# Experts' outputs scattered to rows by token and choice, loaded back by plain transfers

## The chip, the cores and the metric

One core of a Trainium2 chip runs the whole program. The metric is device time in microseconds (us) of one execution; the figure given for a kernel is the median of its timed runs. The engines are PE (matmul), DVE (vector), ACT (scalar), POOL (GpSimd) and SP, which here only issues transfers. All DMA transfers, whichever engine issues them, run on the core's 16 DMA engines; in the profile queue q1 is SP's, q10 ACT's and q0 POOL's.

## What is computed

The reference is one inference step of a two-layer decoder trunk for 288 tokens of 1024 features (256 of a prompt, 8 times 4 of samples), in float32. Layer 0 mixes tokens by attention, layer 1 by a gated short convolution; each mixer is followed by a layer norm of `ALPHA*x + f(x)` and then by a mixture of experts. The change lies in the experts:

```python
g_val, g_idx = lax.top_k(p_group, 1)              # one of 4 groups
e_val, e_loc = lax.top_k(p_exp, EXPERT_TOPK)      # two of its 8 experts
gates = g_val * e_val / sum(e_val)
e_idx = g_idx * EXPERTS_PER_GROUP + e_loc
y[t] = sum over k of gates[t, k] * expert(e_idx[t, k], x[t])
expert(e, x) = (silu(x @ w_gate[e]) * (x @ w_up[e])) @ w_down[e]
```

Each token thus has two expert outputs, 576 rows of 1024 floats (4 KB) in a layer. There are 32 experts; the three matrices of one (1024x512, 1024x512, 512x1024) are 2 MB each.

## The kernel before, in words

**Slots.** Every expert has CAP = 64 slots, so a layer has 32 x 64 = 2048 slots in the first pass, of which the 576 token choices fill 18 on average for an expert. (If an expert gets more than 64 tokens, a branch under `If(full > 0)` runs further passes; it isn't taken here.) A token's slot number is `64*expert + rank`, and SLOTI holds it for six columns: three tiles of tokens (128, 128 and 32) times two choices.

**Rows in.** Two experts form a pair of 128 slots, 16 pairs in a layer. For a pair, DVE builds a 0/1 matrix of tokens by slots (`choose_rows`, L1033), PE multiplies it with the token numbers (L1498), DVE turns the result into indices (`find_rows`, L1052; an empty slot gets an index beyond the table), and POOL gathers the tokens' rows x_rows from DRAM by an indirect transfer of 128 indices (L546); indices beyond the bound are skipped. PE transposes them, ACT evacuates.

**An expert.** PE does gate and up together (L1475, L1478), ACT the silu (L612), DVE the product (L1111), PE a transpose (L1186), DVE its copy (L1116, `ht`), PE the down product (L1490) into one bank: 64 slots by the first 512 outputs in partitions 0 to 63, the other 512 in partitions 64 to 127. PE interleaves: gate and up of expert e, then the down product of e-1, then the transpose of e. ACT's order in a step is silu of e, evacuation of a gathered pair, output of e-1.

**Weights.** SP loads them in program order into three buffers; each load waits until the expert three before has used its buffer (`load_gate_up` L382, its gate load L387, its up load L388; `load_down` L390, load L395).

**Rows out.** ACT copies an expert's bank once, 128x512 (L762; the trace shows the helper's line L609), into one of NYO = 4 buffers YO, and issues two stores of 64x512 floats (128 KB each, L745) to the table slot_out in DRAM, which has a row for each slot, filled or empty. After all stores POOL gathers back, by SLOTI, one row for each token and choice: six indirect transfers (L593) into four buffers YG, the last two after DVE has used the first (`y_used`). Each is preceded by an `If` for the overflow table. DVE accumulates `x += gate * y` twice a tile (L1144), and norms the rows (`norm_rows`); POOL computes the power for it (L532).

**Around it.** In layer 0 SP loads two of six blocks of the convolution's weights when the down product of expert 29 is done (L445), then waits for all six gathers (L447) before it loads the other four.

Of the kernel before, what the change touches and what calls it, by code (L numbers as in the profile page):

```python
# [20 lines left out]
F32 = mybir.dt.float32  # L21
I32 = mybir.dt.int32
# [92 lines left out]
def build_in(nc, t, ctx):  # L115
# [25 lines left out]
    WORK = 9396  # L141
# [7 lines left out]
    SLOTI, SLOTM, SLOTQ, TOKI, IDXC, FLAG = common(6), common(6), common(6), common(3), common(1), common(2)  # L149
    TOKF, IDXG = common(3), common(2)  # L150
    ZERO = common(SLOTS // 128)
# [44 lines left out]
    NYO = 4  # L196
    moe = region(WORK, S0)
    HID, HT, YO, OHP = moe(2, FE), moe(2, FC, CAP), moe(NYO, D // 2), moe(2, 3, 2 * CAP)
# [5 lines left out]
    YG = region(WORK, S0)(4, D)  # L204
# [6 lines left out]
    behind_yg = region(WORK + 4 * D, S0)  # L211
    SCW, SCT, UL = behind_yg(D), behind_yg(DC, 19), behind_yg(DC, 18)
# [6 lines left out]
    table_d = nc.dram_tensor("bias_table", [SHIFTS, 17, TABLE_W], F32).ap()  # L219
    xrows_d = [nc.dram_tensor(f"x_rows{i}", [NTOK, D], F32).ap() for i in range(DEPTH)]  # L220
    slot_tok_d = [nc.dram_tensor(f"slot_token{i}", [SLOTS, 1], I32).ap() for i in range(DEPTH)]
    yslot_d = [nc.dram_tensor(f"slot_out{i}", [NE * CAP, D], F32).ap() for i in range(DEPTH)]
    ymore_d = [nc.dram_tensor(f"slot_more{i}", [SLOTS - NE * CAP, D], F32).ap() for i in range(DEPTH)]
# [28 lines left out]
    st_y = [sem(f"st_y{k}") for k in range(NYO)]  # L252
    ygath = [sem(f"ygath{k}") for k in range(4)]
# [4 lines left out]
    more = [{n: sem(f"more{i}_{n}") for n in ("scat", "w", "tok", "gath", "T", "Tevac", "gu", "silu", "h", "hT", "hTe", "dn", "y", "st", "more")} for i in range(DEPTH)]  # L258
# [34 lines left out]
    def store_count(layer, e):  # L293

        return 32 * (layer * (NE // NYO) + e // NYO + 1)

    NOWHERE = 4096
# [5 lines left out]

    def ygath_count(layer, j):

        return 16 * (layer * (2 if j % 4 < 2 else 1) + j // 4 + 1)


# [28 lines left out]
    def _(sp):  # L337
# [63 lines left out]
        def experts(layer):  # L401
# [12 lines left out]
            with sp.If(full > 0):  # L414
# [8 lines left out]
                sp.wait_ge(s["st"], 32 * n_more)  # L423
            with sp.Else():
                sp.nop()

# [19 lines left out]
        for k in range(4):  # L446
            sp.wait_ge(ygath[k], ygath_count(0, k + 4 if k < 2 else k))  # L447
# [24 lines left out]
    def _(pool):  # L472
        nc.gpsimd.memset(ZERO.bitcast(I32), NTOK).then_inc(zero_set, 1)
        nc.gpsimd.memset(NEGH, -0.5).then_inc(zero_set, 1)
        pool.wait_ge(zero_set, 2)
        nc.gpsimd.iota(TOKI.bitcast(I32), pattern=[[128, 3]], base=0, channel_multiplier=1).then_inc(zero_set, 1)
        pool.wait_ge(zero_set, 3)
        nc.gpsimd.tensor_scalar(TOKF, TOKI.bitcast(I32), float(-NOWHERE), None, ALU.add).then_inc(zero_set, 1)
# [55 lines left out]
        def experts(layer):  # L534
# [7 lines left out]
            for q in range(NPAIR):  # L542
# [5 lines left out]
                    in_offset=bass.IndirectOffsetOnAxis(ap=IDXG[:, q % 2:q % 2 + 1].bitcast(I32), axis=0),  # L548
                    bounds_check=NTOK - 1, oob_is_err=False).then_inc(xr_ld[q % 2], 16)
            pool.wait_ge(xg_T, NPAIR * (layer + 1))  # L550
# [3 lines left out]
            with pool.If(full > 0):  # L554
                for i, (_, n) in enumerate(TILES):
                    for k in range(2):
                        pool.indirect_dma_start(
                            out=slot_tok_d[layer], out_offset=bass.IndirectOffsetOnAxis(ap=SLOTI[0:n, 2 * i + k:2 * i + k + 1].bitcast(I32), axis=0),
                            in_=TOKI[0:n, i:i + 1].bitcast(I32), in_offset=None).then_inc(s["scat"], 16)
                pool.wait_ge(s["scat"], 96)  # L560
                with pool.Fori(1, PASSES) as r:
                    with pool.Fori(0, NE) as e:
                        n = (r - 1) * NE + e
                        pool.wait_ge(s["T"], n)
                        pool.dma_start(IDXC[0:CAP, 0:1].bitcast(I32), slot_tok_d[layer][bass.ds((r * NE + e) * CAP, CAP)]).then_inc(s["tok"], 16)
# [6 lines left out]
                pool.wait_ge(s["st"], 32 * n_more)  # L572
            with pool.Else():
                pool.nop()

            for k in range(NYO):
                pool.wait_ge(st_y[k], 32 * (NE // NYO) * (layer + 1))
            for j in range(6):
                i = STEPS[j // 2]
                n, col = TILES[i][1], 2 * i + j % 2  # L580
                if j >= 4:
                    pool.wait_ge(y_used, 6 * layer + j - 3)
                with pool.If(full > 0):

                    pool.indirect_dma_start(
                        out=YG[0:n, j % 4, :], out_offset=None, in_=ymore_d[layer],
                        in_offset=bass.IndirectOffsetOnAxis(ap=SLOTM[0:n, col:col + 1].bitcast(I32), axis=0),
                        bounds_check=SLOTS - NE * CAP - 1, oob_is_err=False).then_inc(s["more"], 16)
                    pool.wait_ge(s["more"], 16 * (j + 1))
                with pool.Else():  # L590
                    pool.nop()

                pool.indirect_dma_start(  # L593
                    out=YG[0:n, j % 4, :], out_offset=None, in_=yslot_d[layer],
                    in_offset=bass.IndirectOffsetOnAxis(ap=SLOTI[0:n, col:col + 1].bitcast(I32), axis=0),
                    bounds_check=NE * CAP - 1, oob_is_err=False).then_inc(ygath[j % 4], 16)
# [9 lines left out]
    def _(act):  # L606
# [133 lines left out]
        def experts(layer):  # L740
# [46 lines left out]
            for k in range(NYO):  # L787
                act.wait_ge(st_y[k], 32 * (NE // NYO) * (layer + 1))
# [844 lines left out]
```

## Time and profile before

| | us |
|---|---|
| median of 3 timed runs (1528.38 to 1538.88) | 1536.95 |
| the profiled execution | 1526.45 |
| its span, first to last instruction | 1524.8 |

The profile is of one execution. The expert stage of layer 0 runs from about 309 to 788 us of the span, that of layer 1 from about 1001 to 1486 us. Between them lies the convolution. "Idle" in a row is what the engine waited before these instructions, and what ended it. A matmul row's line is that of the kernel; ACT's copies all carry the helper's line L609.

### The profile page before, as it was taken

Reading aid. Unit: us, or ns where it says so; the run is one execution under the profiler, and the core shown is the slowest. Engines: PE = TensorE matmul, PEld = TensorE weight load, DVE = VectorE, ACT = ScalarE, POOL = GpSimd, SP = SyncE. Lnnn points to the kernel's source line nnn. Section 1 sums busy time; section 2 is a strip of 40 time slices with the busy share of each in tenths; the row PEclk is TensorE's granted clock in tenths of the full one; section 3 lists DMA queues with packets and bytes.
Section 4 is the critical chain, followed back from the end, with each engine's and each line's share of the span. In section 5 each row is a group of like instructions: output and inputs, shape, how many; then the busy total and the mean of one; then the engine's idle time right before and its main releaser. Section 6 shows DMA issues by size and latency. Waiting matters only on the chain.

```text
span 1524.8 us, 14763 instructions
## 1 busy us (share of the span) xinstructions
PE 1280.9 (84%) x5744; PEld 588.1 (39%) x5744; DVE 329.7 (22%) x1056; ACT 201.1 (13%) x457; POOL 103.9 (7%) x149
## 2 busy tenths in 40 slices
PE   6999899599988888889864998689989898898880
PEld 4766445333333233233223774333333233333320
DVE  0053525521111111111004323421111111111005
ACT  1123431021111101101000000021101011011100
POOL 4001310100000000000001000000000000000002
PEclk9999999699999999999986999779989999999995
DMA  8740544969999999999989234549999999999973
GB/s 224 197 166 21 166 146 187 374 249 424 420 419 424 420 422 423 420 423 419 425 320 325 79 158 182 207 145 423 419 423 421 419 423 419 424 419 422 421 293 100
DMA packets 100403, 488.33 MB, mean 320 GB/s; under 512 B 14799, under 2 KB 19935, under 8 KB 83948
## 3 DMA queue, kind: packets, MB, share of 16 engines
q1 hardware_dynamic: 80772, 452.70, 73.2%
q0 software_dynamic: 8256, 15.02, 4.1%
q10 hardware_dynamic: 11304, 19.65, 3.5%
q8 instruction: 47, 0.77, 0.2%
q14 instruction: 24, 0.20, 0.0%
HBM read 476.93 MB, written 22.44 MB: 328 GB/s over the span
## 4 chain that ended last, share of the span: by engine, by line
PE 46%; DMA 37%; SPq 7%; DVE 4%; issue 2%; POOL 1%; ACT 1%; POOLq 0%; ACTq 0%; DVEq 0%
DMA mem<-w_exp_up 34%; PE bank L1478 9%; PE bank L1475 7%; SPq L387 7%; PE bank L1591 6%; PE bank L1225 5%; PE bank L1326 4%; PE bank L1490 4%; PE bank L1186 3%; PE bank L1223 1%; DMA mem<-w_attn_in 1%; PE bank L1363 1%; PE bank L1429 1%; ACT mem L609 1%; DMA mem<-slot_out,mem 1%
## 5 line engine op out<-in xcount | busy, mean ns | idle before, releaser
L1478 PE MATMUL bank<-mem 128*64 128x512 f32 x1024 | 500.9, 646 | 97.7 <-DMA mem<-w_exp_up 97.7
L1475 PE MATMUL bank<-mem 128*64 128x512 f32 x1024 | 510.2, 648 | 3.7 <-ACT mem L609 3.0
L1478 PEld LDWEIGHTS bank<-mem 128*64 128x64 f32 x1024 | 146.4, 148 | 362.2 <-issue 220.0
L1490 PE MATMUL bank<-mem 128*64 128x512 f32 x1024 | 240.3, 601 | 2.1 <-DVE mem L1116 2.1
L609 ACT COPY mem<-bank 128x512 f32<-128x512 f32 (+8 forms) x275 | 127.3, 491 | 587.3 <-PE bank L1490 195.6
L1186 PE MATMUL bank<-mem 128*128 128x128 f32 (+4 forms) x798 | 120.4, 285 | 73.3 <-DVE mem L980 37.7
L1111 DVE TENSOR_TENSOR mem<-mem,bank 64x512 f32<-64x512 f32 x64 | 44.3, 692 | 623.6 <-ACT mem L612 623.6
L1475 PEld LDWEIGHTS bank<-mem 128*64 128x64 f32 x1024 | 142.7, 148 | 73.2 <-issue 64.3
L1186 PEld LDWEIGHTS bank<-mem 128*128 128x128 f32 (+4 forms) x798 | 89.6, 165 | 168.5 <-issue 89.1
L612 ACT ACTIVATE mem<-bank 64x512 f32<-64x512 f32 x64 | 37.7, 589 | 638.2 <-PE bank L1478 638.2
L1490 PEld LDWEIGHTS bank<-mem 128*64 128x64 f32 x1024 | 70.3, 137 | 120.8 <-issue 114.4
L1591 PE MATMUL bank<-mem 128*128 128x288 f32 x384 | 95.3, 412 | 0.7 <-ACT mem L609 0.7
L546 POOL DMA_INDIRECT mem<-x_rows,mem x32 | 31.9, 995 | 808.7 <-DVE mem L1057 779.9
L1591 PEld LDWEIGHTS bank<-mem 128*128 128x128 f32 x384 | 74.1, 193 | 21.8 <-ACT mem L609 1.1
L1225 PE MATMUL bank<-mem 128*128 128x288 f32 (+1 forms) x288 | 78.3, 430 | 2.3 <-DMA mem<-w_attn_in 2.3
L1116 DVE COPY mem<-bank 128x256 f32<-128x256 f32 x64 | 27.2, 425 | 208.4 <-PE bank L1186 208.4
L1225 PEld LDWEIGHTS bank<-mem 128*128 128x128 f32 (+1 forms) x288 | 55.6, 197 | 21.5 <-issue 4.1
L1326 PE MATMUL bank<-mem 128*128 128x512 f32 x128 | 61.5, 636 | 0.0
L1498 PEld LDWEIGHTS bank<-mem 128*128 128x128 f32 (+1 forms) x192 | 28.4, 203 | 30.0 <-issue 28.9
L1326 PEld LDWEIGHTS bank<-mem 128*128 128x128 f32 x128 | 25.7, 207 | 30.7 <-issue 30.6
L1498 PE MATMUL bank<-mem 128*128 128x1 f32 (+1 forms) x192 | 31.6, 268 | 6.3 <-DVE mem L1048 6.3
L532 POOL TENSOR_TENSOR mem<-mem 128x1 f32<-128x1 f32 (+1 forms) x12 | 18.1, 1506 | 236.1 <-DVE mem L976 236.0
(172 smaller groups left out, 589.9 us busy)
## 6 DMA issues: line engine op xcount, KB each, us to landing
mem<-w_exp_gate SPq DMA_DIRECT2D x64, 2048.0 KB, 33.6
mem<-w_exp_up SPq DMA_DIRECT2D x64, 2048.0 KB, 31.7
mem<-w_exp_down SPq DMA_DIRECT2D x64, 2048.0 KB, 35.8
slot_out<-mem ACTq DMA_DIRECT2D x128, 128.0 KB, 7.6
mem<-w_conv_in SPq DMA_DIRECT2D x6, 2048.0 KB, 17.8
mem<-w_attn_in SPq DMA_DIRECT2D x5, 2048.0 KB, 16.6
mem<-w_attn_out SPq DMA_DIRECT2D x1, 4096.0 KB, 16.5
mem<-cache_k_a SPq DMA_DIRECT2D x16, 256.0 KB, 2.7
```

Source lines behind the costliest of these rows:

```text
L387: sp.dma_start(WG[k], t["w_exp_gate"][layer, e].rearrange("(p c) f -> p c f", c=DC)).then_inc(ld_wg[k], 16)
L609: return nc.scalar.copy(out, in_)
L612: return nc.scalar.activation(out, in_, ACT.Silu)
L1111: V_.tensor_tensor(h, h, bank[2 + k][CAP:2 * CAP, :], ALU.mult).then_inc(h_done, 1)
L1186: return nc.tensor.transpose(out, in_, ID[0:n, 0:n] if n is not None else ID[CAP:2 * CAP, CAP:2 * CAP])
L1225: last = mm(out[0:n, 0:NTOK], w[:, c, :], XT[:, c, :], start=c == 0, stop=c == DC - 1)
L1326: last = mm(bank[2 * i + half][0:n, :], rows, w[:, c, 512 * half:512 * half + 512], start=c == 0, stop=c == DC - 1)
L1475: mm(out[0:CAP, :], x[:, c, :], wg[:, c, :], start=c == 0, stop=c == DC - 1)
L1478: last = mm(out[CAP:2 * CAP, :], x[:, c, :], wu[:, c, :], start=c == 0, stop=c == DC - 1)
L1490: last = mm(out[CAP * half:CAP * half + CAP, :], h[:, f, :], wd[:, f, 512 * half:512 * half + 512], start=f == 0, stop=f == FC - 1)
L1498: last = mm(bank[q % 2][:, 0:1], OHP[0:n, q % 2, j, :], TOKF[0:n, j:j + 1], start=j == 0, stop=j == 2)
L1591: last = mm(bank[3 * (j % 2) + part][:, 0:NTOK], w[:, c, 128 * (j % 4):128 * (j % 4) + 128], XT[:, c, :], start=c == 0, stop=c == DC - 1)
```

## The change

Instead of storing every slot, the kernel writes only the filled slots' rows, to a table y_rows with a row for each token and choice, by an indirect transfer from POOL with 128 indices for each pair; empty slots get an index beyond the bound and are left out. For this the one-hot matrix holds 1 for a first choice and 2 for a second, and PE multiplies it with two columns (token number less an offset, and 1), so that DVE can tell the choice (HITS) and derive both the index to gather and the row to write (IDXY). ACT copies an expert's bank in two halves so that a pair's 128 slots lie in 128 partitions with 4 KB each, in two buffers YP. POOL's scatters follow its gathers with a lag of three pairs. Back come six plain loads from SP into six buffers YG, with no branch; the table is in token order. SLOTM, the overflow table and its gathers go; the overflow branch scatters too. The convolution's small inputs SCW move into free partitions of X, as YG takes their place.

The core of the diff:

```diff
-    YG = region(WORK, S0)(4, D)
+    YG = region(WORK, S0)(6, D)
...
+    ROW0, ROW1, NROWS, NOWHERE = 2 * NTOK + 1, 1, 3 * NTOK + 1, 4 * NTOK + 1
...
+    def token_rows(table, k, lo, n):
+        if k == 0:
+            return table[ROW0 + lo:ROW0 + lo + n]
+        return table[ROW1:ROW1 + 2 * NTOK].rearrange("(t two) d -> t two d", two=2)[lo:lo + n, 0, :]
...
+        def load_outputs(layer):
+            for k in range(NYP):
+                sp.wait_ge(st_y[k], store_count(layer, NPAIR - NYP + k))
+            for j in range(6):
+                i = STEPS[j // 2]
+                lo, n = TILES[i]
+                sp.dma_start(YG[0:n, j, :], token_rows(yrows_d[layer], j % 2, lo, n)).then_inc(ld_y[j], 16)
...
         load_conv(0, (0, 1))
-        for k in range(4):
-            sp.wait_ge(ygath[k], ygath_count(0, k + 4 if k < 2 else k))
+        load_outputs(0)
         load_conv(0, (2,))
         load_conv(1)
...
         experts(1)
+        load_outputs(1)
...
-            for q in range(NPAIR):
+            def gather(q):
                 Q = NPAIR * layer + q
                 pool.wait_ge(ix_ready, Q + 1)
                 wait(pool, xg_T, Q - 1)
                 pool.indirect_dma_start(
...
+            def scatter(q):
+                pool.wait_ge(y_evac, base + 2 * q + 2)
+                pool.indirect_dma_start(
+                    out=yrows_d[layer], out_offset=bass.IndirectOffsetOnAxis(ap=IDXY[:, q:q + 1].bitcast(I32), axis=0),
+                    in_=YP[:, q % NYP, :], in_offset=None,
+                    bounds_check=NROWS - 1, oob_is_err=False).then_inc(st_y[q % NYP], 16)
+            LAG = 3
+            for q in range(NPAIR):
+                gather(q)
+                if q >= LAG:
+                    scatter(q - LAG)
+            for q in range(NPAIR - LAG, NPAIR):
+                scatter(q)
...
-            for k in range(NYO):
-                pool.wait_ge(st_y[k], 32 * (NE // NYO) * (layer + 1))
-            for j in range(6):
...
-                pool.indirect_dma_start(
-                    out=YG[0:n, j % 4, :], out_offset=None, in_=yslot_d[layer],
-                    in_offset=bass.IndirectOffsetOnAxis(ap=SLOTI[0:n, col:col + 1].bitcast(I32), axis=0),
-                    bounds_check=NE * CAP - 1, oob_is_err=False).then_inc(ygath[j % 4], 16)
...
                 act.wait_ge(dn_psum, E + 1)
-                wait(act, st_y[b], store_count(layer, e) - 32)
-                copy(YO[0:2 * CAP, b, :], bank[6 + k][0:2 * CAP, :]).then_inc(y_evac, 1)
-                act.wait_ge(y_evac, E + 1)
-                store(e * CAP, yslot_d[layer], YO[0:2 * CAP, b, :], st_y[b])
+                wait(act, st_y[q % NYP], store_count(layer, q) - 16)
+                for half in range(2):
+                    last = copy(YP[CAP * k:CAP * k + CAP, q % NYP, 512 * half:512 * half + 512],
+                                bank[6 + k][CAP * half:CAP * half + CAP, :])
+                last.then_inc(y_evac, 1)
...
-            wait(dve, xr_ld[q % 2], row_loads(layer, q) - 16)
-            V_.tensor_scalar(IDXG[:, q % 2:q % 2 + 1].bitcast(I32), bank[q % 2][:, 0:1], float(NOWHERE), None,
-                             ALU.add).then_inc(ix_ready, 1)
+            found = bank[q % 2]
+            link(V_.tensor_scalar(HITS[:, q:q + 1], found[:, 1:2], -0.5, 1.5, ALU.mult, ALU.add))
+            V_.tensor_scalar(IDXG[:, q:q + 1].bitcast(I32), found[:, 0:1], HITS[:, q:q + 1], float(2 * NTOK), ALU.mult, ALU.add)
+            V_.tensor_scalar(IDXY[:, q:q + 1].bitcast(I32), found[:, 0:1], float(NOWHERE), None, ALU.add).then_inc(ix_ready, 1)
...
-                    last = mm(bank[q % 2][:, 0:1], OHP[0:n, q % 2, j, :], TOKF[0:n, j:j + 1], start=j == 0, stop=j == 2)
+                    last = mm(bank[q % 2][:, 0:2], OHP[0:n, q % 2, j, :], TOKF[0:n, j, :], start=j == 0, stop=j == 2)
```

`store_count(layer, q)` is 16 for each scatter of a pair's buffer so far; DVE's accumulates wait for `ld_y[j]` of their own load.

## Rows read from the trace of the kernel before

**Rows 1.** The page: the chain's shares by line, and the convolution's matmul group.

```profile
DMA mem<-w_exp_up 34%; PE bank L1478 9%; PE bank L1475 7%; SPq L387 7%; PE bank L1591 6%; PE bank L1225 5%; PE bank L1326 4%; PE bank L1490 4%; PE bank L1186 3%; PE bank L1223 1%; DMA mem<-w_attn_in 1%; PE bank L1363 1%; PE bank L1429 1%; ACT mem L609 1%; DMA mem<-slot_out,mem 1%
...
L1591 PE MATMUL bank<-mem 128*128 128x288 f32 x384 | 95.3, 412 | 0.7 <-ACT mem L609 0.7
```

**Rows 2.** The chain in order of time: start us, us, what.

```profile
351.65 3.58 PE bank L1490 x16
...
363.49 3.58 PE bank L1490 x16
...
1128.48 8.55 SPq L387
...
1176.28 8.34 SPq L387
```

**Rows 3.** DMA, 333 to 772 us; the last row is of 1027 to 1468 us.

```profile
DMA  9999999999999999999999999999999999999999
...
q1 hardware_dynamic: 22759, 175.22, 95.5%
q10 hardware_dynamic: 4640, 7.61, 4.6%
q0 software_dynamic: 1872, 1.77, 1.2%
...
slot_out<-mem ACTq DMA_DIRECT2D x59, 128.0 KB, 7.6
...
mem<-x_rows,mem POOLq DMA_INDIRECT x13, 9.8
...
q10 hardware_dynamic: 4660, 7.65, 4.6%
```

**Rows 4.** Windows after a gather, between gathers: busy, PE clock, DMA, GB/s.

```profile
451.00:461.00 10.00, 8.57 (x42) 2.76 (x40) 0.42 (x1) 0.58 (x1) 0.82 (x1) 1.00 1.02 415
...
461.00:482.00 21.00, 18.14 (x80) 6.71 (x78) 3.67 (x11) 2.84 (x5) 0.00 (x0) 0.92 1.02 425
```

**Rows 5.** DMA, 1000 to 1085 us: GB/s in 40 slices of 2.1 us.

```profile
GB/s 0 8 0 0 0 77 254 424 422 428 430 46 116 247 432 426 412 411 396 420 436 436 424 465 409 380 413 414 465 418 434 409 421 387 420 439 438 431 434 431
```

**Rows 6.** The chain in order of time: both tails, a first gather.

```profile
301.29 3.48 DMA mem<-x_rows,mem
...
787.61 0.59 ACT mem L609
...
802.47 1.30 DVE mem L1144
...
1484.92 0.59 ACT mem L609
...
1498.24 1.30 DVE mem L1144
```

**Rows 7.** The timeline at the first index of layer 0: start, us.

```profile
300.20 0.14 DVE L1057 TENSOR_SCALAR mem<-bank 128x1 int32<-128x1 f32 x1
```

**Rows 8.** DMA issues of the whole run: KB each, us to landing.

```profile
mem<-x_prompt SPq DMA_DIRECT2D x1, 1024.0 KB, 6.9
...
new_v_a_prompt<-mem SPq DMA_DIRECT2D x1, 512.0 KB, 2.8
...
mem<-slot_out,mem POOLq DMA_INDIRECT x12, 4.5
```

**Rows 9.** The timeline of one step of layer 1: start, us, idle before.

```profile
1117.01 0.99 POOL L546 DMA_INDIRECT mem<-x_rows,mem  x1 [30.48 <-DVE mem L1057]
...
1119.18 0.59 ACT L609 COPY mem<-bank 128x512 f32<-128x512 f32 x1 [3.85 <-PE bank L1490]
...
1119.56 0.42 DVE L1116 COPY mem<-bank 128x256 f32<-128x256 f32 x1 [3.32 <-PE bank L1186]
```

**Rows 10.** Waits, 450 to 740 us: total us, times, longest.

```profile
POOL mem L546 <- DVE mem L1057: 273.5, 9, 30.7
ACT mem L612 <- PE bank L1478: 193.6, 18, 13.7
```

More of the change, by code:

```diff
@@ L140, in build_in @@
     S0 = TOTAL - 3 * SLOT
-    WORK = 9396
+    WORK = 9536
     common = region(0, WORK)
@@ L251, in build_in @@
     xr_ld = [sem(f"xr_ld{k}") for k in range(2)]
-    st_y = [sem(f"st_y{k}") for k in range(NYO)]
-    ygath = [sem(f"ygath{k}") for k in range(4)]
+    st_y = [sem(f"st_y{k}") for k in range(NYP)]
+    ld_y = [sem(f"ld_y{j}") for j in range(6)]
     x_alpha, y_used, pe_passed, pool_passed = sem("x_alpha"), sem("y_used"), sem("pe_passed"), sem("pool_passed")
@@ L257, in build_in @@
         sem("cv_" + n) for n in ("in_T", "in", "psum", "h", "u", "z", "lT", "lsb"))
-    more = [{n: sem(f"more{i}_{n}") for n in ("scat", "w", "tok", "gath", "T", "Tevac", "gu", "silu", "h", "hT", "hTe", "dn", "y", "st", "more")} for i in range(DEPTH)]
+    more = [{n: sem(f"more{i}_{n}") for n in ("scat", "w", "tok", "gath", "T", "Tevac", "gu", "silu", "h", "hT", "hTe", "dn", "y", "st")} for i in range(DEPTH)]
     def linker(eng, own):
@@ L472, in _ @@
     def _(pool):
-        nc.gpsimd.memset(ZERO.bitcast(I32), NTOK).then_inc(zero_set, 1)
+        nc.gpsimd.memset(ZERO.bitcast(I32), NOWHERE).then_inc(zero_set, 1)
         nc.gpsimd.memset(NEGH, -0.5).then_inc(zero_set, 1)
         pool.wait_ge(zero_set, 2)
-        nc.gpsimd.iota(TOKI.bitcast(I32), pattern=[[128, 3]], base=0, channel_multiplier=1).then_inc(zero_set, 1)
+        nc.gpsimd.memset(TOKF, 1.0)
+        for k, (row, step) in enumerate(((ROW0, 1), (ROW1, 2))):
+            nc.gpsimd.iota(TOKI[:, k, :, 0].bitcast(I32), pattern=[[128, 3]], base=0, channel_multiplier=1)
+            last = nc.gpsimd.iota(TOKI[:, k, :, 1].bitcast(I32), pattern=[[128 * step, 3]], base=row, channel_multiplier=step)
+        last.then_inc(zero_set, 1)
         pool.wait_ge(zero_set, 3)
-        nc.gpsimd.tensor_scalar(TOKF, TOKI.bitcast(I32), float(-NOWHERE), None, ALU.add).then_inc(zero_set, 1)
+        nc.gpsimd.tensor_scalar(TOKF[:, :, 0], TOKI[:, 0, :, 0].bitcast(I32), float(-2 * NTOK), None, ALU.add).then_inc(zero_set, 1)
         for layer in range(DEPTH):
@@ L571, in experts @@
                             bounds_check=NTOK - 1, oob_is_err=False).then_inc(s["gath"], 16)
[L572 removed]
+                        pool.wait_ge(s["y"], n + 1)
+                        pool.sem_inc(pool_passed, 1)
+                        pool.indirect_dma_start(
+                            out=yrows_d[layer], out_offset=bass.IndirectOffsetOnAxis(ap=IDXC[0:CAP, 1:2].bitcast(I32), axis=0),
+                            in_=YP[0:CAP, 0, :], in_offset=None,
+                            bounds_check=NROWS - 1, oob_is_err=False).then_inc(s["st"], 16)
+                        pool.wait_ge(s["st"], 16 * (n + 1))
+                        pool.sem_inc(pool_passed, 1)
             with pool.Else():
                 pool.nop()
[L576 to L596 removed]
             rstd(2 * layer + 1)
@@ L741, in experts @@
             base = NE * layer
-            def store(row0, table, y, done):
-                for h in range(2):
-                    act.dma_start(table[bass.ds(row0, CAP), 512 * h:512 * h + 512], y[CAP * h:CAP * h + CAP]).then_inc(done, 16)
             def gathered(i, v):
@@ L786, in experts @@
             full = act.value_load(FLAG[0:1, layer:layer + 1].bitcast(I32), min_val=0, max_val=1)
-            for k in range(NYO):
-                act.wait_ge(st_y[k], 32 * (NE // NYO) * (layer + 1))
+            for k in range(NYP):
+                act.wait_ge(st_y[k], store_count(layer, NPAIR - NYP + k))
             with act.If(full > 0):
@@ L797, in experts @@
                         act.wait_ge(s["dn"], n + 1)
-                        act.wait_ge(s["st"], 32 * n)
-                        copy(YO[0:2 * CAP, 0, :], bank[6][0:2 * CAP, :]).then_inc(s["y"], 1)
-                        act.wait_ge(s["y"], n + 1)
-                        store(n * CAP, ymore_d[layer], YO[0:2 * CAP, 0, :], s["st"])
-                act.wait_ge(s["st"], 32 * n_more)
+                        for half in range(2):
+                            last = copy(YP[0:CAP, 0, 512 * half:512 * half + 512], bank[6][CAP * half:CAP * half + CAP, :])
+                        last.then_inc(s["y"], 1)
+                act.wait_ge(s["st"], 16 * n_more)
             with act.Else():
```

57 lines of the change are left out of this document (24 added, 33 removed).

## The prediction, made before the change was run

> **What bounds the kernel now.** I read the chain that ended last first. 34% of the span is one thing, the wait for w_exp_up; no matmul line has over 9% [rows 1]. In order of time the chain has a repeating pattern in the expert stage: the last gate matmul frees a weight buffer, SP issues the next gate load, and PE waits for the up load behind it. From one such release (1128.48) to the next (1176.28) are 47.8 us for the three experts whose buffers turn once, so 15.9 us an expert [rows 2]. Early in a stage, while preloaded weights last, PE sets the pace: 363.49 - 351.65 = 11.84 us an expert [rows 2]. So for most of the stage the weights come 4 us an expert too slowly.
>
> Whether that is latency or traffic is told by the DMA view of that stretch. From 333 to 772 us (layer 0) every slice of the DMA busy row is 9, and the loads' queue q1 takes 95.5% of the 16 engines, ACT's queue q10 4.6%, POOL's q0 1.2%: the engines are full, and the three shares add to 101.3% [rows 3]. Layer 1, from 1027 to 1468 us, has the same 4.6% on q10 [rows 3]. In such a stretch time is work of the DMA engines; taking work off them shortens it, until PE's 11.84 us would bind, which 4 us an expert keeps far away.
>
> **Part 1: the stores of whole slots go.** In 333 to 772 us ACT issued 59 stores slot_out of 128 KB, live or empty, 7.61 MB on q10, at 4.6% of 439 us = 20.2 us, or 19.9 us after dividing by 1.013 [rows 3]. By bytes, at the 423 GB/s between gathers [rows 4], it is 18.0 us. I take 19.9, since it was measured on the queue itself. That these bytes displace loads is seen just before the first store of layer 1: four full slices of 422 to 430 GB/s with q1 nearly alone [rows 5], against 175.22 MB in 439 us = 399 GB/s for q1 beside the stores [rows 3].
>
> **Part 2: the scatters come.** One per pair of experts: 59 / 4 = 14.75 pairs, of which 14 scatters land in the stretch. No scatter is in this trace; the nearest row is the gather of x_rows, also 128 indices of 4 KB rows, and also mostly empty. 13 gathers moved 1.77 MB on q0, 136 KB each = 33 live rows, not 512 KB: empty rows cost no row's bytes there [rows 3]. Two prices come from it. By share: 1.2% of 439 us / 13 / 1.013 = 0.40 us. By rate: in the 10 us after each gather's issue the total was 410 to 415 GB/s (nine such windows, mean 413.6, the first shown), in the rest between them 421 to 425 (nine, mean 422.9, the first shown) [rows 4]; 9.3 GB/s over 10 us are 93 KB, 0.22 us lost beside the gather's own 136 KB / 423 = 0.32 us, together 0.54 us. I take 0.55, for the scatter keeps as many software-made transfers in flight as the gather: 14 x 0.55 = 7.7 us. It can't be below nothing, because it moves bytes that must be moved. Its upper end is what it costs if empty rows travel too, the rival below.
>
> The Trainium skill (DMA: Bandwidth & Descriptors, Latency and other measured facts) speaks against this part: it says that engines 7 and 15 are usually slower and gives, as its best guess, the rings of software-made descriptors that all engines fetch. The 413.6 against 422.9 GB/s agree in sign [rows 4], though nothing here shows which engine. With the rule a scatter keeps the 0.22 us; without it, at 0.32 us, 28 scatters would be 6.4 us cheaper.
>
> Net in layer 0: 19.9 - 7.7 = 12.2 us; by the lowest store price and this scatter 18.0 - 7.7 = 10.3, by the highest difference of shares 19.9 - 5.6 = 14.3. Layer 1 has the same rows, so both: **-24.4 us** (-20.6 to -28.6), 0.44 us of the 15.9 us an expert.
>
> **Part 3: the tail of each layer.** Now, in layer 1: copy of the last output ends 1484.92 + 0.59 = 1485.51, then come its store and POOL's four If blocks and gathers, whose second lands for DVE's second accumulate at 1498.24; in layer 0, 788.20 to 802.47 [rows 6]. After: a second copy (+0.58), POOL's start, which took 0.9 us before a layer's first gather (index written at 300.34, gather at 301.29), and a scatter as long as that unloaded gather, 3.48 us [rows 6, 7]: 1485.51 + 0.58 + 0.9 + 3.48 = 1490.5. Then SP issues plain loads. The second must land for the 1498.24 step. A 512 KB transfer from SP took 2.8 us, x_prompt's 1 MB 6.9 us at the crowded start [rows 8]; two issues of 0.4 us and 1 MB I put at 4.5 us, between these: 1495.0. Gain 3.2 us (0.8 to 4.4). Layer 0 still has conv weights in the engines, so I take the scatter at the 4.5 us of the slot_out gathers [rows 8]: 788.20 + 0.58 + 0.9 + 4.5 + 4.5 = 798.7 against 802.47, gain 3.8 (1.4 to 5). Behind that the chain is DVE's arithmetic, and the later gathers were hidden under it; nothing more is won. Both layers: **-7.0 us**. SP's four conv loads of layer 0 are queued behind the y loads and start sooner than behind today's wait for all gathers; conv's matmuls idled 0.7 us in all, for ACT and not for these loads [rows 1], so that gains nothing; if they share the engines with the y loads, layer 0 loses up to 2.5 us of its gain (1 MB more at 423 GB/s).
>
> The Trainium skill (DMA: Bandwidth & Descriptors, Anatomy of one DMA) prices a software-issued transfer at about 2.0 us and bytes over 436 GB/s. As an estimate that is 2.3 us for the last scatter, and both tails would be some 3 us shorter still; the measured 3.48 us of the gather stands against it.
>
> **Part 4: small things on the path or under cover.** find_rows becomes three small DVE operations with one own wait. Before the first gather of a layer this is on the chain: 0.14 us becomes three times that and a wait between, about 0.54 [rows 7], **+0.4 us** a layer. Later it stands between h's multiply and the copy of ht, where DVE waits 3.32 us for PE anyway [rows 9]. ACT copies twice 64x512 instead of once 128x512: +0.59 us an expert less the issue of two stores; its cover is 193.6 / 18 = 10.8 us an expert of waiting for PE [rows 10]. Were that cover gone, 0.59 us would cost 38 us in 64 experts.
>
> POOL is in order: scatter(q-3) waits for the copy of its pair's second expert with gather(q+1) queued behind. In a steady step POOL issues the gather at 1117.01, and the output copy of the expert before ends 1119.18 + 0.59 [rows 9]. So gather(q) leaves first, scatter(q-3) follows some 4 us later in the same step, and the next gather is not due for 30 us (POOL waited 273.5 us in 9 gathers) [rows 10]. The buffer is next needed three steps later, 47.8 us; a scatter would have to take over 40 us to hold ACT, and gathers took 9.8 at the median [rows 3]. POOL's longer prologue lies under the first attention weights, and the dropped SLOTM arithmetic on no path.
>
> **Sum.** -24.4 - 7.0 + 0.8 = -30.6 us on the profiled execution's 1526.45 us (span 1524.8): 1495.85, a factor 0.980. The median of the runs is 1536.95, 0.7% above the profiled one; by the same factor it becomes 1506.1. I predict **1506 us**. Its own range is 1499 to 1515: the best ends of parts 2 and 3 give -28.6 - 9.4 + 0.8 = -37.2, the worst -20.6 - 2.2 + 0.8 = -22.0.
>
> **Rivals.**
> *The stores ride free.* They leave SBUF where loads enter it; if that direction alone is full, removing them frees nothing and only the tail remains: -6.2, 1520.25, as a median 1531. For it: ACT's stores are only 4.6%. Against: q1's 399 GB/s beside stores and over 422 without them [rows 3, 5]. Chance 0.11.
>
> *Empty rows travel, slower than before.* A scatter that carries all 128 rows at the gather's price per live row costs 0.55 x 128 / 33 = 2.13 us; 14 are 29.8 us against 19.9 removed: +9.9 a layer, less 6.2 in tails and starts: 1540.05, as a median 1551. It decides from (19.9 + 3.1) / 14 = 1.64 us a scatter on. For it: no indexed write is in the trace, and the bounds test is on the written side now. Against: the gathers' 136 KB [rows 3]. Chance 0.06.
>
> *A costly but not ruinous scatter*, 1.0 to 1.4 us by more drag: net 0 to 6 us a layer, 1508 to 1520, as a median 1518 to 1530. Chance 0.07.
>
> **How the numbers follow.** My forecast has 0.76. Median runs of before spread over 0.7%, and the profiled execution lies at their low end, so an after at 1496 is as much this case as 1506. For 8 in 10 I take 1490 to 1530: up to the free stores, without the slower rival. About 1%, 15 us, is what a measurement of this kernel can tell from no change. Faster by more (below 1521.6): the forecast and a part of the costly scatter, 0.81. Within 1%: free stores and the rest, 0.13. Slower: 0.06.
>
> **What would show it.** Right: q10 nearly empty in the expert stretches, q0 at about 2.5% with some 270 KB for each pair, q1 near 411 GB/s, DMA still full; 46.5 us instead of 47.8 for three experts; from the start of the last output copy to the second accumulate 11.1 us in layer 0 (now 14.9) and 10.1 in layer 1 (now 13.3). Wrong: q0 at 600 KB a pair (empty rows travel), q1 still at 399 with idle engines (stores were free), ACT or PE waiting for a scatter, or y loads landing later than 6 us after the scatter.

## The result, and the profile after

| | before | after |
|---|---|---|
| median of the runs shown with the result (4 of each) | 1534.67 us | 1511.19 us (1507.62 to 1517.46) |
| ratio, 95% interval | | 0.986 [0.9815, 0.9905] |
| the profiled execution | 1526.45 us | 1517.46 us |

The change makes the kernel 1.4% faster, 2.0% was forecast: 1506 predicted, 1511 measured. The page after:

```profile
DMA mem<-w_exp_up 34%; PE bank L1481 9%; PE bank L1478 8%; SPq L387 7%; PE bank L1594 6%; PE bank L1228 5%; PE bank L1493 4%; PE bank L1329 4%; PE bank L1189 4%; PE bank L1226 2%; DMA mem<-w_attn_in 1%; PE bank L1277 1%; PE bank L1259 1%; PE bank L1366 1%; PE bank L1432 1%
...
L1594 PE MATMUL bank<-mem 128*128 128x288 f32 x384 | 95.2, 412 | 0.7 <-ACT mem L620 0.7
```

The kernel is still bound by the weight loads (w_exp_up keeps its 34% of the chain), and the convolution's matmuls idle the same 0.7 us as in [rows 1]: moving its four loads had no effect that shows here. A window of the DMA view in the steady part of layer 0 (queue, packets, MB, share of the 16 engines), first of before, then of after:

```profile
q1 hardware_dynamic: 17771, 136.07, 95.8%
q10 hardware_dynamic: 3464, 5.69, 4.4%
```

```profile
q1 hardware_dynamic: 18099, 139.92, 98.8%
q0 software_dynamic: 3024, 2.79, 2.4%
...
y_rows<-mem POOLq DMA_INDIRECT x11, 10.9
```

Both are of 420 to 760 us. q10 is gone, q0 is at the forecast 2.4%, and q1 rose from 136.07 / 340 us = 400.2 GB/s to 139.92 / 340 = 411.5; the prediction said 411. The eleven scatters and ten gathers moved 2.79 MB together, 133 KB each, far from the 512 KB of 128 rows: empty rows don't travel.

The chain of after in order of time (start us, us, what): the first gather, SP's waits for a free weight buffer, and the tail, for both layers:

```profile
311.38 3.38 DMA mem<-x_rows,mem
...
793.90 0.49 ACT mem L620
...
795.84 3.16 DMA y_rows<-mem
...
799.45 6.02 DMA mem<-y_rows
...
805.57 1.29 DVE mem L1147
...
997.53 4.19 DMA mem<-x_rows,mem
...
1098.03 8.10 SPq L387
...
1424.22 7.87 SPq L387
...
1477.54 0.47 ACT mem L620
...
1479.48 2.63 DMA y_rows<-mem
...
1482.59 5.74 DMA mem<-y_rows
...
1488.42 1.30 DVE mem L1147
```

Three things are read here. From 1098.03 to 1424.22 lie seven turns of three experts, 46.60 us each (46.5 forecast). The tail from the last output's copy to the second accumulate is 11.67 us in layer 0 and 10.88 in layer 1, against 14.86 and 13.32 in [rows 6]. And layer 0 begins at 311.38 where before began at 301.29. That last one isn't the change's: in the attention, which is the same code, PE ran at a granted clock of 0.68 (1 is full speed) in this execution and of 0.94 in that of before, and in another execution of the kernel after layer 0 begins at 300.42 (experiment 1). The clocks are in these windows (busy us of PE, PEld, DVE, ACT, POOL, then the clock, DMA share, GB/s; before, then after):

```profile
140.00:195.00 55.00, 47.33 (x252) 29.86 (x252) 25.04 (x116) 22.62 (x79) 19.34 (x43) 0.94 0.52 156
```

```profile
140.00:195.00 55.00, 50.63 (x212) 30.96 (x211) 25.54 (x120) 19.64 (x75) 12.40 (x27) 0.68 0.32 93
```

So the span as a whole is a poor ruler for this change. A better one is cut out of the chain, in each layer: the **stretch**, from the start of the first gather to the start of the last output's copy, and the **tail**, from there to the start of the second accumulate. It repeats: another execution of the unaltered kernel after gives the same stretches within 0.4 us (experiment 1).

The stretch still holds PE's clock at its two ends. A finer ruler lies inside the part in which the weights set the pace: from SP's issue of the fifth load of a w_exp_down in a stretch to its issue of the 28th, the last but one; 23 experts lie between. I call it **between the marks**. The two executions of the kernel after differ there by 0.03 us or less. SP's timeline at the marks of layer 0, then of layer 1, first of before, then of after_again:

```profile
379.19 0.38 SPq L395 DMA_DIRECT2D mem<-w_exp_down  x1
...
742.91 1.07 SPq L395 DMA_DIRECT2D mem<-w_exp_down  x1
...
1075.87 0.38 SPq L395 DMA_DIRECT2D mem<-w_exp_down  x1
...
1437.79 3.89 SPq L395 DMA_DIRECT2D mem<-w_exp_down  x1
```

```profile
381.13 0.38 SPq L395 DMA_DIRECT2D mem<-w_exp_down  x1
...
736.44 1.41 SPq L395 DMA_DIRECT2D mem<-w_exp_down  x1
...
1067.24 0.38 SPq L395 DMA_DIRECT2D mem<-w_exp_down  x1
...
1422.03 1.54 SPq L395 DMA_DIRECT2D mem<-w_exp_down  x1
```

All kernels of this study by these rulers, us:

| kernel | stretch, layer 0 | stretch, layer 1 | between the marks, layers 0 and 1 | tail, layer 0 | tail, layer 1 | ratio to before |
|---|---|---|---|---|---|---|
| before | 486.3 | 490.6 | 363.7, 361.9 | 14.9 | 13.3 | 1 |
| after, first profile | 482.5 | 480.0 | 355.3, 354.8 | 11.7 | 10.9 | 0.986 |
| after_again | 482.2 | 480.0 | 355.3, 354.8 | 11.6 | 11.4 | 0.9879 |
| stores_back | 499.5 | 497.5 | 371.4, 371.3 | 13.6 | 11.7 | 1.0125 |
| scatter_twice | 489.1 | 489.5 | 363.2, 363.4 | 16.1 | 12.2 | 1.0032 |
| empty_rows | 486.1 | 486.7 | 362.6, 361.9 | 14.7 | 12.5 | 0.9999 |
| narrow | 496.9 | 494.4 | 368.7, 367.1 | 15.1 | 11.3 | 1.0081 |
| spread | 475.6 | 475.0 | 350.4, 350.1 | 12.8 | 10.7 | 0.979 |
| spread_staged | 475.6 | 475.1 | 350.1, 350.0 | 11.9 | 9.3 | 0.9785 |
| before_spread | 484.6 | 487.0 | 361.4, 359.0 | 15.0 | 13.8 | 0.9955 |
| lag1 | 501.4 | 502.7 | 355.0, 355.2 | 11.2 | 10.8 | 1.0181 |

### The profile page after: what moved, and what is told of

Same layout as the page of the kernel before. It is cut to its first block, busy times and chain, and to the rows that moved or that the text cites. A ratio compares the mean times of both kernels' runs of the same rounds, so it can differ in the third digit from the quotient of the medians.

```text
span 1515.8 us, 14759 instructions
## 1 busy us (share of the span) xinstructions
PE 1289.5 (85%) x5744; PEld 590.4 (39%) x5744; DVE 336.8 (22%) x1112; ACT 238.0 (16%) x521; POOL 125.7 (8%) x173
## 4 chain that ended last, share of the span: by engine, by line
PE 48%; DMA 37%; SPq 7%; DVE 5%; issue 2%; ACT 1%; POOL 1%; POOLq 0%; DVEq 0%; ACTq 0%
DMA mem<-w_exp_up 34%; PE bank L1481 9%; PE bank L1478 8%; SPq L387 7%; PE bank L1594 6%; PE bank L1228 5%; PE bank L1493 4%; PE bank L1329 4%; PE bank L1189 4%; PE bank L1226 2%; DMA mem<-w_attn_in 1%; PE bank L1277 1%; PE bank L1259 1%; PE bank L1366 1%; PE bank L1432 1%
## 5 line engine op out<-in xcount | busy, mean ns | idle before, releaser
L620 ACT COPY mem<-bank 128x512 f32<-128x512 f32 (+7 forms) x339 | 164.2, 507 | 593.1 <-PE bank L1493 194.5
L566 POOL DMA_INDIRECT y_rows<-mem x32 | 32.1, 1002 | 226.9 <-ACT mem L620 226.9
## 6 DMA issues: line engine op xcount, KB each, us to landing
mem<-w_attn_out SPq DMA_DIRECT2D x1, 4096.0 KB, 16.6
```

The lines of the kernel that those rows point to most:

```text
L620: return nc.scalar.copy(out, in_)
```

## The experiments

Ratios are to the kernel before, run beside each kernel on the same chip (medians 1529 to 1531 us); differences between ratios are turned to microseconds with 1529. One per cent is 15 us.

**1. The kernel after once more**, unaltered, as the base for the rest.

> The changed kernel unaltered, for a narrower interval and a second profile. The sum of the prediction says a ratio of 0.980; the four runs so far gave 0.986. If the shortfall is only PE's clock in the one profiled execution, the ratio comes near 0.980; if 2 us a layer in the price of the stores, 2 us a layer in uneven engines and 0.7 us a tail are really missing, it stays at 0.985 to 0.988. q1 should carry 411 to 412 GB/s in the full stretches either way.

Measured: 1511.62 us, 0.9879 [0.9836, 0.9922], so -18.5 us. The chain of this profile:

```profile
300.42 3.53 DMA mem<-x_rows,mem
...
782.63 0.49 ACT mem L620
...
794.19 1.30 DVE mem L1147
...
986.03 4.15 DMA mem<-x_rows,mem
...
1465.99 0.47 ACT mem L620
...
1477.35 1.30 DVE mem L1147
```

Here layer 0 begins at 300.42, close to before. Its profiled execution took 1506.39 us, 20.1 less than before's, and of that -14.8 us lie in the stretches (-4.1 and -10.6) and -5.3 in the tails (-3.3 and -2.0). The ratio is near the upper end of what the expectation gave for terms that are really missing, not near 0.980, so the shortfall is not PE's clock in the first profile alone.

**2. The stores put back** into the kernel after, beside the scatters: ACT issues the two 128 KB stores of each expert again, to a table that nobody reads, and YP's reuse waits for them too. This prices the stores alone.

```diff
+                act.wait_ge(y_evac, E + 1)
+                for half in range(2):
+                    act.dma_start(dump_d[layer][e * CAP:e * CAP + CAP, 512 * half:512 * half + 512],
+                                  YP[CAP * k:CAP * k + CAP, q % NYP, 512 * half:512 * half + 512]).then_inc(st_d[q % NYP], 16)
```

> The changed kernel, and ACT also stores every expert's whole 64 slots again (two stores of 128 KB an expert, to a table that nobody reads). Theory: stores displace loads byte for byte, 18.1 to 19.9 us in a full stretch of 440 us, so about +38 us for both layers against the changed kernel, above the kernel before (ratio about 1.010), q1 back at 393 to 397 GB/s. Rival, stores ride free: no change against the changed kernel (ratio 0.986), q1 stays at 411 GB/s beside them.

Measured: 1548.84 us, 1.0125 [1.0071, 1.0178]: 37.6 us above after_again. DMA view, 420 to 760 us, and the chain:

```profile
q1 hardware_dynamic: 17471, 134.68, 94.7%
```

```profile
300.72 3.51 DMA mem<-x_rows,mem
...
800.20 0.58 ACT mem L623
...
1006.57 4.37 DMA mem<-x_rows,mem
...
1504.06 0.58 ACT mem L623
```

q1 falls to 134.68 / 340 = 396.1 GB/s. The rival that stores ride free is excluded: they cost 17.3 us of stretch in layer 0 and 17.5 in layer 1, and 2.3 us of the two tails. Between the marks they cost 16.1 and 16.5. The prediction had 19.9 a layer from the queue's share, and 18.0 by bytes; the bytes were nearer. ACT waited for no store in 450 to 740 us, so this is the stores' price and not that of the added wait.

**3. Each pair scattered twice**, the second time to a table that nobody reads.

```diff
+                pool.indirect_dma_start(
+                    out=dump_d[layer], out_offset=bass.IndirectOffsetOnAxis(ap=IDXY[:, q:q + 1].bitcast(I32), axis=0),
+                    in_=YP[:, q % NYP, :], in_offset=None,
+                    bounds_check=NROWS - 1, oob_is_err=False).then_inc(st_y[q % NYP], 16)
```

> The changed kernel, and each pair's rows are scattered a second time, to a second table that nobody reads: the price of a scatter, measured by doubling it. By the prediction's 0.55 us, 28 more in the full stretches are 15.4 us, and 1 us more in each tail: +17 us (ratio near 0.999). By bytes and the skew of the engines that spread and narrow showed: 28 x 0.37 us of bytes and 4 to 5 us of skew a layer, +18 to +20 us (1.000). If a scatter were as dear as the empty-rows rival said, 2.13 us, +60 us (1.027). If it were free, 0.988.

Measured: 1535.74 us, 1.0032 [1.0005, 1.0058]: 23.4 us above after_again, more than expected. By the ruler 6.9 and 9.6 us lie in the stretches and 5.4 in the tails, where the second of the last two scatters runs behind the first. Per scatter of the stretch (28, by the prediction's count) that is 16.5 / 28 = 0.59 us by the profiles, and (23.4 - 5.4) / 28 = 0.64 by the medians. Between the marks the cost is 7.9 and 8.6 us. The prediction took 0.55. A costly scatter of 1.0 to 1.4 us is excluded.

**4. Empty slots written too**, each to a spare row of its own, 512 KB a pair. DVE gets one more small operation for each pair and some columns of constants.

```diff
-                    bounds_check=NROWS - 1, oob_is_err=False).then_inc(st_y[q % NYP], 16)
+                    bounds_check=ALLROWS - 1, oob_is_err=False).then_inc(st_y[q % NYP], 16)
...
+            link(V_.tensor_scalar(SPARE[:, q:q + 1], HITS[:, q:q + 1], 1.25, SPOT[:, q:q + 1], ALU.is_gt, ALU.mult))
+            V_.tensor_scalar(IDXY[:, q:q + 1].bitcast(I32), found[:, 0:1], SPARE[:, q:q + 1], float(NOWHERE), ALU.add, ALU.add).then_inc(ix_ready, 1)
```

> The changed kernel, but the empty slots are not left out: each gets a row of its own behind the table, so that every scatter writes all 128 rows (512 KB for a pair instead of some 150). The words left out in the change are undone, the rest stays. By bytes a scatter then costs 0.524 MB / 423 GB/s = 1.24 us, evenly over the engines: 28 x (1.24 - 0.37) = +24 us, less the scatters' share of the skew, 4 to 5 us a layer: +14 to +20 us (ratio 0.997 to 1.001), so the forecast's rival of 2.13 us a scatter (ratio 1.017 or more) would be too dear even if empty rows did travel. If leaving the empty slots out were worth nothing, 0.988.

Measured: 1531.04 us, 0.9999 [0.9967, 1.003], 18.4 us above after_again; the whole gain of the change is gone. DMA view, 420 to 760 us:

```profile
q0 software_dynamic: 3004, 7.01, 5.2%
...
y_rows<-mem POOLq DMA_INDIRECT x11, 12.4
```

7.01 MB on q0 against 2.79 of after: this is what the trace looks like when empty rows travel, so in the kernel after they do not. The surprise is in the stretches: 1472 empty rows of 4 KB a layer are 6.0 MB, 14.3 us at 423 GB/s, and the stretches grew by 3.9 and 6.7 us only. Between the marks, without PE's clock at the start, it is 7.3 and 7.1 us, still about half. My reading is that such cheap bytes went to engines that had time left; experiments 5 to 7 test it.

**5 and 6. Other partitions for the same rows.** A token of rank r in its expert sits in slot r, in partition r or 64 + r, so the rows that travel crowd in the low partitions of each half: the fullest expert has 29 tokens in layer 0 and 39 in layer 1, the mean is 18. Nothing but the columns of the one-hot matrix is renumbered. spread puts rank r at 4*(r mod 16) + r div 16, a new group of four partitions for each of the first 16 ranks; narrow packs the ranks into few such groups, in pairs 32 partitions apart.

```diff
-    c[:, C_IOTA:C_IOTA + 128] = np.arange(128)
+    c[:, C_IOTA:C_IOTA + NE] = np.arange(NE)
+    r = np.arange(CAP)
+    at = 4 * (r % 16) + r // 16
+    c[:, C_PAIR + at] = r
+    c[:, C_PAIR + CAP + at] = CAP + r
```

In narrow the third added line of code is another:

```diff
-    at = 4 * (r % 16) + r // 16
+    at = 4 * (r // 8) + r % 4 + 32 * (r // 4 % 2)
```

> The changed kernel with another numbering of the 64 slots of an expert: rank r sits in slot 4*(r mod 16) + r div 16 instead of slot r, by another constant row in the one-hot comparison; no instruction more or less. The filled slots, 18 of 64 on average, then lie in all groups of four partitions and not in the first five. Theory, the row transfers load the DMA engines unevenly: by the split of partitions over engines that the Trainium skill gives (DMA: Bandwidth and Descriptors, The descriptor swizzle) the busiest engine has 64 to 70 live rows a layer now and 45 then, against a mean of 36; as an estimate the skew of gather and scatter falls from 9 to 10 us a layer to 3 us, and 6 to 14 us of the whole would go (ratio 0.977 to 0.982). Rival, a fixed drag of software-made descriptors whatever partition they serve: no change (ratio 0.986), and the windows after a gather stay 9 GB/s below the others.

> The opposite numbering: rank r sits in slot 4*(r div 8) + r mod 4 + 32*((r div 4) mod 2), so that the first eight ranks lie in partitions 0 to 3 and 32 to 35, which by the Trainium skill (DMA: Bandwidth and Descriptors, The descriptor swizzle) belong to one engine. Theory, uneven engines: the busiest engine then has 126 to 128 live rows a layer against 64 to 70 now, and as an estimate 18 us more a layer if all of it counts, half of that if faster engines run ahead: +18 to +36 us against the changed kernel (ratio 0.998 to 1.010), and longer landings of scatters and gathers. Rival, a fixed drag per software-made transfer: no change (0.986).

Measured: spread 1497.06 us, 0.979 [0.9745, 0.9836], 13.6 us below after_again; narrow 1542.0 us, 1.0081 [1.0049, 1.0112], 30.9 us above. The same transfers, the same rows, the same bytes, and 45 us between the two. DMA view of spread, 420 to 760 us, its chain, then narrow's DMA view:

```profile
q1 hardware_dynamic: 18151, 139.90, 98.8%
```

```profile
302.06 3.32 DMA mem<-x_rows,mem
...
777.70 0.49 ACT mem L624
...
981.75 3.66 DMA mem<-x_rows,mem
...
1456.75 0.47 ACT mem L624
```

```profile
q1 hardware_dynamic: 17732, 136.55, 97.7%
```

narrow shows it in the rate, 136.55 / 340 = 401.6 GB/s. spread does not: q1 moves 139.90 MB, as in after, and yet both stretches are 6.6 and 5.0 us shorter. My reading: the rate is a sum over 16 engines, a load has landed when the last of them is done, and the engines with fewer rows run ahead in the meantime. In narrow they seem to run out of room for it: between two gathers the total was 422 GB/s at 441 to 459 us and 391 at 666 to 684. The expected longer landings came only for a gather that is alone (the first of layer 0: 4.45 us in narrow, 3.53 in after_again, 3.32 in spread); under load they hardly moved (scatters 11.0 us at the median in narrow against 10.9 in after, gathers 10.2 against 9.9).

The Trainium skill (DMA: Bandwidth & Descriptors, The descriptor swizzle) gives for a transfer to 128 partitions the engine 8 * (partition >> 6) + ((partition >> 2) & 7), by which the two numberings were made. The page says it of the partitions that a transfer writes; that an indirect transfer, and a scatter that reads them, is split alike is assumed. By it and the routing of these inputs the fullest engine carries 64 live rows in layer 0 and 70 in layer 1 in each direction in the kernel after, 45 and 45 in spread, 128 and 126 in narrow, where the mean is 36. As an estimate from that page and the 423 GB/s of [rows 4], shared by 16 engines, a row more on the fullest engine costs 4 KB / 26.4 GB/s = 0.155 us; gather and scatter together make that 13.7 us less for spread and 37 us more for narrow. The stretches gave -11.5 and +29.2: the sign and the order agree, the size is eight tenths. The same estimate fits two other runs: in empty_rows the fullest engine goes from 64 and 70 rows a layer to 128 in the scatters, which makes 9.9 and 9.0 us, and in scatter_twice it gets 64 and 70 more, 9.9 and 10.9 us; between the marks they gave 7.3 and 7.1, 7.9 and 8.6, seven to eight tenths again. No view here shows a single engine, so which ones they are rests on the page alone; that the partition matters is what the runs show.

**7. The kernel before, with spread's numbering**, so that only its gathers are spread (the reading back follows the new numbers; seven small DVE operations a layer off the path). Is the crowding the change's own?

```diff
+            link(V_.scalar_tensor_tensor(SLOTF, RK, 3.0, SLOTF, ALU.mult, ALU.add))
+            for r in range(1, 4):
+                link(V_.tensor_scalar(QQ, RK, 16.0 * r, -63.0, ALU.is_ge, ALU.mult))
+                link(V_.tensor_tensor(SLOTF, SLOTF, QQ, ALU.add))
```

> The kernel before with spread's numbering of the slots, for its gathers; the index for reading back follows by seven small DVE operations off the path. The gathers of the kernel before lie on the same few partitions as those of the changed kernel, its stores fill all slots. Theory, uneven engines: gather and scatter share the skew of the changed kernel half and half, so the kernel before gains half of the 13 us that spread gained: -5 to -8 us (ratio 0.995 to 0.997), and the change itself brought the other half. Rival: gathers into SBUF are not slowed by it, and all the skew came with the scatters: no change (1.000), so that the change had 13 us of new cost.

Measured: 1525.32 us, 0.9955 [0.9927, 0.9983], -6.9 us (-11.2 to -2.6), about half of the 13.6 us that the same numbering gave the kernel after; between the marks it is 5.3 us for both layers against 9.6. So the rival, no change, is excluded, and by the middle of a wide interval half of the crowding was there before, in the gathers, and the change brought the other half, some 6.7 us, by adding scatters from the same partitions, in place of stores of all slots alike.

One thing the spreading did not change is the dip in the rate after a gather's issue, from which the prediction took 0.22 us [rows 4]. Here it is in before_spread, after a gather at 453.88 and then up to the next:

```profile
454.00:464.00 10.00, 6.57 (x24) 1.95 (x22) 0.42 (x1) 0.58 (x1) 0.88 (x1) 0.80 1.01 413
464.00:486.00 22.00, 22.00 (x98) 7.95 (x96) 3.67 (x11) 2.83 (x5) 0.00 (x0) 0.94 1.02 425
```

That is 413 against 425 GB/s, as before (415 against 425). So the dip is not the crowding, and what it costs stays open.

**8. The scatter one pair behind the gathers instead of three.**

```diff
-            LAG = 3
+            LAG = 1
```

> The changed kernel with the scatters one pair behind the gathers instead of three, so that in POOL's queue the next gather waits behind a scatter that waits for ACT. Theory: POOL's order is covered either way in the stretches where the weights set the pace, the gather still leaves a step before it is needed: same as the changed kernel (0.986 to 0.990). Rival: the queue matters, each gather comes a step or two later and PE waits for rows, some us a layer in the early steps of 11.84 us (0.990 to 1.000).

Measured: 1558.0 us, 1.0181 [1.0139, 1.0222], 46 us above after_again, where I had expected no change. Stretches of 501.4 and 502.7 us. Waits of lag1, 450 to 740 us (total us, times, longest), and POOL's timeline:

```profile
POOL y_rows L566 <- ACT mem L620: 287.7, 10, 30.5
...
PE bank L1189 <- DMA mem<-x_rows,mem: 48.7, 9, 6.1
```

```profile
424.86 1.00 POOL L566 DMA_INDIRECT y_rows<-mem  x1 [29.01 <-ACT mem L620]
426.17 1.02 POOL L559 DMA_INDIRECT mem<-x_rows,mem  x1 [0.30 <-issue]
```

The same two views of the kernel after:

```profile
POOL mem L559 <- DVE mem L1065: 236.8, 9, 28.0
...
ACT mem L623 <- PE bank L1481: 177.2, 18, 13.1
```

```profile
430.70 1.01 POOL L559 DMA_INDIRECT mem<-x_rows,mem  x1 [23.50 <-DVE mem L1065]
434.52 1.01 POOL L566 DMA_INDIRECT y_rows<-mem  x1 [2.81 <-ACT mem L620]
```

With a lag of three POOL waits for the index, the gather leaves first and the scatter 3.8 us later, as Part 4 of the prediction read it from [rows 9]. With a lag of one POOL stands at the scatter, which waits for ACT, and the gather behind it is held with its index long ready. It leaves right behind the scatter, takes its 9 to 10 us under load, and PE's transposes wait for it at every pair. They cost time in the first experts: from the first gather to the fifth down load 100.0 and 101.3 us pass in the two layers against 80.7 and 81.2 in after_again, while between the marks both kernels take 355 us. There PE waits for rows (48.7 us in 450 to 740) in place of w_exp_up (35.9 in after, nothing in lag1); whether it is more than chance that the two come out alike isn't shown. So the rival had the right place, the early steps, but 19 to 20 us a layer where it said some us, and the expected equality holds only between the marks. The 46 us are the price of the order, not of the scatter: the eleven scatters of 420 to 760 us landed sooner here than in after (8.7 us at the median against 10.9).

**9. spread, with the first tile's two loads ahead of the other four.**

```diff
             for j in range(6):
+                if j == 2:
+                    sp.wait_ge(ld_y[0], 16 * (layer + 1))
+                    sp.wait_ge(ld_y[1], 16 * (layer + 1))
```

> The slot numbering of spread, and the six loads of the outputs in two parts: SP issues the first tile's two, waits for both, then issues the other four. Theory: the second load now shares the engines with the four behind it (5.7 to 6.0 us from its issue to landing for 1 MB ahead of it); alone it would land after 3.5 to 4 us, so each tail loses 2 us, and the later tiles still come before they are needed: -4 us against spread (ratio 0.976). Rival: the landing is latency and not sharing: same as spread (0.979).

Measured: 1499.76 us, 0.9785 [0.9748, 0.9823], not told apart from spread. In its profile the tails are shorter by 0.9 and 1.4 us, where 2 were expected: the sign is that of loads that share the engines, but it is below what the runs resolve.

## Why the prediction was right, and where its sum was off

The mechanism held at each step that had a sign: engines full before and after, q10 gone, q0 at 2.4%, q1 at 411.5 GB/s, 46.6 us for three experts, empty rows left out, ACT and PE waiting for no scatter in the steady part. 1511 lies in the range, on the side of a smaller gain. The sum, by profiles of like kernels (layers added):

| term | forecast | measured | from |
|---|---|---|---|
| stores removed | -39.8 | -34.8 | stores_back less after_again, stretches |
| scatters added | +15.4 | +16.5 | scatter_twice less after_again, stretches |
| tails | -7.0 | -5.3 | after_again less before, tails |
| first index of a layer | +0.8 | +0.7 | layer 1: 990.64 to 994.31 before, 993.51 to 997.53 after; twice that |
| sum | -30.6 | -22.9 | |
| the two kernels' profiled executions | | -20.1 | 1506.39 less 1526.45 |
| ratio of the medians | | -18.5 [-25.1, -11.9] | after_again |

**The term that failed is the price of the stores**: "I take 19.9, since it was measured on the queue itself". The stores, added to the kernel after, took 17.4 us a layer, near the 18.0 that the prediction had worked out from the bytes and set aside. That is 5.0 of the 7.7 us between the two sums. My reading, which no run tests apart, is that a queue's share counts time in which its packets shared the engines with other packets.

**The tails** were mis-sized by 1.7 us in their last step. The last scatter landed in 3.16 and 2.63 us (4.5 and 3.48 forecast), sooner than thought; the second load landed 6.02 and 5.74 us after its issue, where I had 4.5. All six loads are issued together and share the engines, to which the 5.00 us points that the same load takes in layer 0 of experiment 9, when the other four wait, against 5.93 in spread. The Trainium skill's estimate for the scatter (DMA: Bandwidth & Descriptors, Anatomy of one DMA), 2.3 us in the prediction, was nearer in layer 1 than the gather's 3.48; the measured 2.63 is between them.

**The scatters** were right in size, 0.59 to 0.64 against 0.55, but not for the reason given. I had put 0.22 of the 0.55 us to a drag of software-made transfers, with the Trainium skill's guess on engines 7 and 15 (same page, Latency and other measured facts) beside it. spread issues the same number of them and is 13.6 us faster, so a good part of the surplus over the bytes is the crowding, while the dip from which I had read the 0.22 us is still there when gathers are spread (experiment 7). That 0.55 came near was luck in part: one cause was priced and another found. By the page's formula engines 7 and 15 get the fewest live rows here (0 and 1 in layer 0, 7 and 9 in layer 1), so a drag on those two would have been easiest to hide.

**The path and the cover** held. Layer 1's first index to gather went from 3.67 to 4.02 us. ACT's extra copy stayed hidden: it waited 177.2 us for PE in 18 experts, 9.8 each, against 10.8 in [rows 10]. "46.5 instead of 47.8" hit its number by luck, for 47.8 was one turn of seven: over the whole steady part of layer 1 before, 1083.27 to 1428.96 us for 22 experts, three took 47.1. One interval of a jittering chain is no mean, and a good part of layer 1's 10.6 us is not in this rate: 0.5 us a turn over 10.7 turns is 5.7 us. Another 3.6 us came in one step, from the fifth to the sixth down load: 15.4 us before, 11.8 in after_again, so the weights kept up with PE for one expert more.

**The two layers, and what stays open.** Between the sum of the terms, -22.9, and the profiles' -20.1 lie 2.8 us. In the stretches layer 0 gained 6.3 us less than its two terms make (4.1 against 17.3 - 6.9) and layer 1 gained 2.7 more (10.6 against 17.5 - 9.6). The marks settle most of that. Between them the kernel after gained 8.4 and 7.1 us, and its two terms make 16.1 - 7.9 = 8.2 and 16.5 - 8.6 = 7.9. The rest of the difference between the layers lies at the two ends, and there PE's clock differed. At the start of layer 0 it was 0.74 in before and 0.68 in after_again (290 to 330 us), and the first output was done 21.2 us after the first gather against 24.0, a head start of 2.8 us for before, which is still 2.8 us at the first mark. From the landing of the last up load to the last output's copy layer 0 took 15.2 us in before and 16.9 in after_again, layer 1 16.6 and 15.2; in the first 5 us of these the clock was 1.00, 0.66, 0.70 and 1.00, that is, in the longer ones PE began, after its wait for that load, at the lower of its two levels, 1.2 and 2.4 GHz (matmuls of 0.85 us and not 0.43). No run sets the clock alike, and a second scatter need not cost just what a first does. Why crowding costs only some eight tenths of the estimate isn't settled: it counts every row of a layer, also those that travel while PE sets the pace, but no run separates the two.

The best version is spread, 1497.06 us: it is faster than both kernels of this case, by 2.1% against before.

## What to carry to other kernels

Where the DMA engines are full, price a removed transfer that uses all partitions alike by its bytes at the full rate, and not by its queue's share of busy time. Bytes that go by few partitions cost more than their share, and the rate of a window need not show it: lay the live rows of an indirect transfer over all partitions. On an in-order engine that issues both, let the transfer that is needed soon go ahead of the one whose data comes late; the lag that does this was worth 46 us here, most of it in the first experts of a layer. To compare two executions, measure between two marks inside the part that one thing limits, so that PE's clock elsewhere stays out.

## What the runs showed of the hardware that was not expected

- The partition of a row sets what its transfer costs the rest: with the same transfers and bytes, 1497.06 us with rows spread over the partitions, 1511.62 with rows in the low ones, 1542.0 with rows packed further.
- Writing 6.0 MB a layer more, of empty rows, most of them in the partitions with few live rows, took only 7.3 and 7.1 us between the marks (3.9 and 6.7 by the stretches), where the full rate of 423 GB/s would give 14.3 for all of them.
- An indirect scatter of 128 indices, some 36 of them live, landed in 2.6 to 3.2 us at a layer's end and in 10.9 us at the median beside the weight loads, and cost these 0.59 to 0.64 us.
